# Modulation vector: four column quarters on the partitions

## Chip, cores and metric

The kernel runs on one core of one Trainium2 chip. The metric is device time in microseconds (us) from start to end of one launch, as the median of several runs; lower is better. Everything is fp32 at the interface.

## What is computed

Two transformer blocks on x of 256 tokens by 2048 features. The first has compressed, selected and windowed attention, a feed-forward layer of width 8192 and a gated embedding; the second has sliding-window and latent attention and again a feed-forward layer of width 8192. The second block is modulated by a conditioning vector c of 2048 elements. The part that the change touches:

```python
c_act = jax.nn.silu(c)                       # (1, 2048)
mod = c_act @ w_mod[l] + b_mod[l]            # w_mod: (2048, 6 * 2048), 96 MB
sh1, sc1, g1, sh2, sc2, g2 = [m[:, None, :] for m in jnp.split(mod, 6, axis=-1)]
h = rmsnorm(x, attn_norm_g[l]) * (1.0 + sc1) + sh1
...
x = x + g1 * jnp.einsum('bsm,md->bsd', mix, w_out[l])
h = rmsnorm(x, mlp_norm_g[l]) * (1.0 + sc2) + sh2
u = jax.nn.relu(jnp.einsum('bsd,df->bsf', h, w_ff1[l]))
x = x + g2 * jnp.einsum('bsf,fd->bsd', u * u, w_ff2[l])
```

`mod` does not depend on x, so its 96 MB of weights are read and summed during the first block, beside that block's matrix products.

## The kernel before

Each of the five engines has a program of its own, written by hand in the order in which it runs; semaphores order them against each other. There is no scheduler. SP (SyncE) issues nearly all loads, ACT and VectorE prepare the weights, TensorE (PE) multiplies.

**Weights of the products.** SP loads units of 1 MB (four blocks of 128 rows by 512 columns, rows of 2 KB) into four slots `raw`. A unit is two steps. For each step ACT copies 128x1024 elements to the rounded type (`upper`, L498) and VectorE subtracts that from the original (`lower`, L912), so that a product of two fp32 matrices can be made from three products of rounded halves. PE waits for `lower_ready`, multiplies a step (L1519 to L1521 in the form "tokens", L1530 and L1535 in the form "columns") and increments `step_used`, which frees the buffer of `upper` and `lower` four steps on. So ACT and VectorE run at most four steps ahead of PE. A product of 2048x512 weights is a group of 8 steps; SP loads the unit for a slot as soon as VectorE has made both `lower` halves of the unit that lay in it.

**The modulation.** w_mod is cut in 96 units of 128 rows by 2048 columns, 16 for each of the six sections. SP issues two units in a group of the first block, behind the third and the fourth load of `raw` (`mod_unit`, L313), alternately into the two slots of `modraw`; before that it waits until the unit two back has been added. VectorE adds a unit behind two of its eight `lower` operations (`add_mod`): the whole `modacc` of 128x2048 is multiplied by a pointer scalar of `silu_c` and added (L926; L924 for the first unit of a section, without the addition). After sixteen units `modacc` holds, on partition p, the sum over the rows with that p, for all 2048 columns of the section. PE turns it (`sum_mod`, L1594: 16 transposes of 128x128, called between two steps of a group of tokens), and VectorE sums the rows of the turned blocks in PSUM (`store_mod`, L939: two reduces of 128x1024), adds the bias (L942) and has the section as 128 partitions by 16 columns in `modcol`. One of the six sections is finished behind the first block's first products, four in its feed-forward layer and the gate, the last one in the second block's first products.

The groups with modulation work are 8 of the first product, 4 of w_out, 32 of the feed-forward layer and 4 of the gate: 48 groups, two units each. In the gate groups VectorE has more besides: `gated` and `regained` (L1333 to L1351) lie in its order between two `lower` operations, and an addition right behind them.

**The start.** Nine vectors (gains, c, b_mod) and two position tables are loaded as rows into `vrow`; PE turns them with three transposes (L1602) and VectorE copies the columns to `vcol` (L1093, L1094), from which `silu_c` is made.

Of the kernel before, what the change touches and what calls it, by code (L numbers as in the profile page):

```python
# [25 lines left out]
P = 128  # L26
# [26 lines left out]
MODS = 6 * KC  # L53

# [30 lines left out]
def program(nc, a):  # L85
    with ExitStack() as ctx:
# [36 lines left out]
        modacc = place("modacc", [P, D], at=M + 16384)  # L123
# [61 lines left out]
        COL = dict(mix=0, ffn=16, ple=32, attn=48, mlp=64, c=80, q=96, kv=99, b=P, k=P + 96, v=2 * P)  # L185
# [103 lines left out]
        def _(sp):  # L289
# [41 lines left out]
            for t in range(T):  # L331
                sp.dma_start(h[:, t, :], a["x"][0, t * P:(t + 1) * P, :]).then_inc(x_landed[t], 16)
            vecs = [(a["norm_mix"][0], 0, 0), (a["norm_ffn"][0], 16, 0), (a["norm_ple"][0], 32, 0),
                    (a["attn_norm_g_2"][0], 48, 0), (a["mlp_norm_g_2"][0], 64, 0), (a["c_2"][0], 80, 0),
                    (a["mla_q_norm_g_2"][0], 96, 0), (a["mla_kv_norm_g_2"][0], 99, 0),
# [5 lines left out]
            sp.dma_start(vrow[0:32, 2, :], a["nsa_cmp_pos_v"][0]).then_inc(rows_landed, 16)  # L341

# [3 lines left out]
            with loop(sp, c, 5, {lower_ready: 8, mod_added: 2}) as i:  # L346
                group(w_in, i * NW + 2 * NW, mods=section_rows(i * 2 + 4, 0))
# [16 lines left out]
            with loop(sp, c, NG - 1, {lower_ready: 8, mod_added: 2}) as i:  # L364
                group(w_out, i * NW + NW, mods=section_rows(i * 2 + 2, 1))
# [14 lines left out]
            with loop(sp, c, QUARTERS - 1, {lower_ready: 64, mod_added: 16}) as i:  # L380
# [3 lines left out]
            with loop(sp, c, NG, {lower_ready: 8, mod_added: 2}) as i:  # L384
                group(w_gate, i * NW, mods=section_rows(i * 2 + 8, 5))
# [91 lines left out]
        def _(act):  # L477
# [164 lines left out]
            nc.scalar.activation(silu_c[:], vcol[:, COL["c"]:COL["c"] + KC], ACT.Sigmoid).then_inc(c_sigmoid, 1)  # L642
# [253 lines left out]
        def _(dve):  # L896
# [19 lines left out]
            def add_mod(k):  # L916

                slot = st["mod"] % 2
                dve.wait_ge(mod_landed[slot], c.next(mod_landed[slot], 16))
                if st["mod"]:  # L920
                    dve.wait_ge(mod_added, c.at(mod_added))
                w, s = modraw[:, slot, :], silu_c[:, bass.ds(k, 1)]
                if isinstance(k, int) and k == 0:
                    op = nc.vector.tensor_scalar(modacc[:], w, s, None, ALU.mult)  # L924
                else:
                    op = nc.vector.scalar_tensor_tensor(modacc[:], w, s, modacc[:], ALU.mult, ALU.add)  # L926
                op.then_inc(mod_added, 1)
                c.next(mod_added)
                st["mod"] += 1

            def store_mod(m):
# [161 lines left out]
            nc.vector.tensor_copy(vcol[:, 0:100], ps[:, 0, 0:100])  # L1093
            nc.vector.tensor_copy(vcol[:, P:], ps[:, 0, P:2 * P + CMP_LEN]).then_inc(cols_ready, 1)  # L1094
# [4 lines left out]
            link(nc.vector.tensor_tensor(silu_c[:], silu_c[:], vcol[:, COL["c"]:COL["c"] + KC], ALU.mult))  # L1099
# [12 lines left out]
            def heads_out(parity, i):  # L1112
# [3 lines left out]
            per = {"steps": 16, "groups": 2, upper_ready: 16, half_copied: 2, mod_added: 4,  # L1116
                   mod_landed[0]: 32, mod_landed[1]: 32}
# [182 lines left out]
            def ffn(gain, modulated):  # L1300
# [6 lines left out]
                if modulated:  # L1307
                    per[dve_step] = 1
                    per.update({mod_landed[0]: 128, mod_landed[1]: 128, mod_added: 16, mod_summed: 1})
# [181 lines left out]
        def _(pe):  # L1491
# [109 lines left out]
            for j, n in ((0, 100), (1, P), (2, CMP_LEN)):  # L1601
                op = nc.tensor.transpose(ps[:, 0, j * P:j * P + n], vrow[0:n, j, :], ident[0:n, 0:n])  # L1602
# [9 lines left out]
            def sums_and_bias():  # L1612
                sum_mod(KC)
# [229 lines left out]
            def ffn(norms, modulated):  # L1843
                def between():
                    sum_mod(c.at("mods", 0))
# [40 lines left out]
            group(tokens, xs, n=320, between={1: lambda: sum_mod(6 * KC), 4: turn_modulation})  # L1886
# [127 lines left out]
```

## Time and profile before

| what | us |
|---|---|
| median of 3 runs (2274.2 to 2277.11) | 2275.6 |
| the profiled execution | 2274.36 |
| its span, first to last instruction | 2272.7 |
| PE busy in the span | 2202.8 |
| VectorE (DVE) busy in the span | 1512.4 |
| ACT busy in the span | 1012.2 |

The profile is of one execution. Its own time is 1.66 us above its span and 1.24 us below the median. PE is the matmul queue of TensorE, PEld its weight loads, which overlap; DVE is VectorE. In an entry of the timeline the first number is the start in us from the span's start, the second the duration of the entry (of all its instructions, where it ends in xN), and in square brackets stands how long the engine had been idle and what released it. "granted clock" is the share of TensorE's full clock; it is 0.991 in the mean.

### The profile page before, as it was taken

To read this page: it belongs to the slowest core of one execution; us is meant where nothing else is said; L and a number is where in the kernel's file an instruction comes from. 1 tells how busy PE (TensorE), PEld (TensorE's weight loads), DVE (VectorE), ACT (ScalarE), POOL (GpSimd) and SP (SyncE) were. 2 spreads that over 40 slices of the span, in tenths; PEclk is the share of its full clock that TensorE was granted. 3 is DMA by queue.
4 is the path that set the end of the run, shared out by engine and by line. 5 is a ranking of instruction groups with operands and counts; after the bars stand their busy time and mean duration, and the time that the engine had idled before them with its cause. 6 is when DMAs were issued, how large, how long until landed. Compare 5 with 4: busy or idle time off the path is not lost.

```text
span 2272.7 us, 29448 instructions
## 1 busy us (share of the span) xinstructions
PE 2202.8 (97%) x11458; PEld 1883.6 (83%) x11458; DVE 1512.4 (67%) x1456; ACT 1012.2 (45%) x1262; POOL 15.1 (1%) x40
## 2 busy tenths in 40 slices
PE   7999999999999999999999898999999999999997
PEld 6888888788888888888878697887888888888886
DVE  6676566777777677767778865557555555655655
ACT  5443364544344344344355544545444443443442
POOL 1000000000000000000000000000000000000000
PEclk9999999999999999999999999999999999999999
DMA  8775508777887877877867353355556656556553
GB/s 323 292 277 180 168 1 315 245 274 287 285 276 280 300 253 265 299 270 279 303 231 279 121 192 112 125 191 151 183 204 182 192 201 186 186 188 200 184 196 120
DMA packets 213106, 499.67 MB, mean 220 GB/s; under 512 B 10068, under 2 KB 12680, under 8 KB 199800
## 3 DMA queue, kind: packets, MB, share of 16 engines
q1 hardware_dynamic: 211528, 491.16, 63.3%
q0 software_dynamic: 1456, 6.72, 0.8%
q8 instruction: 96, 1.57, 0.3%
q14 instruction: 26, 0.21, 0.0%
HBM read 495.68 MB, written 2.17 MB: 219 GB/s over the span
## 4 chain that ended last, share of the span: by engine, by line
PE 60%; issue 36%; DVE 2%; ACT 1%; DMA 0%; SPq 0%; POOL 0%; DVEq 0%; ACTq 0%; POOLq 0%
PE ps L1530 17%; PE ps L1519 9%; PE ps L1520 9%; PE ps L1521 9%; PE ps L1535 9%; PE ps L1711 2%; PE ps L1767 1%; PE ps L1577 1%; PE ps L1630 1%; PE ps L1594 0%; PE ps L1717 0%; ACT prob L707 0%; PE ps L1768 0%; PE ps L1765 0%; DMA raw<-in_nsa_w_in_dram 0%
## 5 line engine op out<-in xcount | busy, mean ns | idle before, releaser
L912 DVE TENSOR_TENSOR lower<-raw,upper 128x1024 fp32r<-128x1024 f32 (+2 forms) x733 | 884.0, 1216 | 523.7 <-ACT upper L498 520.4
L498 ACT ACTIVATE upper<-raw 128x1024 fp32r<-128x1024 f32 (+2 forms) x733 | 769.0, 1054 | 951.8 <-PE ps L1521 529.2
L1530 PE MATMUL ps<-xs,upper 128*128 128x512 f32 x2688 | 676.1, 394 | 4.6 <-DVE h L1002 4.2
L1530 PEld LDWEIGHTS ps<-xs,upper 128*128 128x128 f32 x2688 | 484.7, 189 | 92.6 <-issue 5.0
L1519 PE MATMUL ps<-upper,hidden 128*128 128x512 f32 x1024 | 399.4, 390 | 0.0
L1520 PE MATMUL ps<-lower,hidden 128*128 128x512 f32 x1024 | 398.7, 389 | 0.0
L1521 PE MATMUL ps<-upper,hidden 128*128 128x512 f32 x1024 | 398.7, 389 | 0.0
L1535 PEld LDWEIGHTS ps<-xs,lower 128*128 128x128 f32 x2688 | 367.7, 191 | 26.3
L1535 PE MATMUL ps<-xs,lower 128*128 128x256 f32 x2688 | 375.7, 283 | 0.0
L1519 PEld LDWEIGHTS ps<-upper,hidden 128*128 128x128 f32 x1024 | 192.3, 188 | 40.3 <-DVE lower L912 0.9
L1521 PEld LDWEIGHTS ps<-upper,hidden 128*128 128x128 f32 x1024 | 192.3, 188 | 39.9
L1520 PEld LDWEIGHTS ps<-lower,hidden 128*128 128x128 f32 x1024 | 192.3, 188 | 39.4
L926 DVE SCALAR_TENSOR_TENSOR modacc<-modraw,silu_c,modacc 128x2048 f32<-128x2048 f32 x90 | 211.2, 2347 | 0.4
L1519 PE MATMUL ps<-upper,xs 128*128 128x512 f32 (+1 forms) x512 | 200.4, 391 | 3.1 <-DVE lower L912 1.9
L1521 PE MATMUL ps<-upper,xs 128*128 128x512 f32 (+1 forms) x512 | 198.0, 387 | 0.0
L1520 PE MATMUL ps<-lower,xs 128*128 128x512 f32 (+1 forms) x512 | 197.8, 386 | 0.0
L1519 PEld LDWEIGHTS ps<-upper,xs 128*128 128x128 f32 x512 | 96.7, 189 | 24.5 <-issue 4.1
L1521 PEld LDWEIGHTS ps<-upper,xs 128*128 128x128 f32 x512 | 96.6, 189 | 19.4
L1520 PEld LDWEIGHTS ps<-lower,xs 128*128 128x128 f32 x512 | 96.7, 189 | 18.2
L525 ACT ACTIVATE half<-ps 128x1024 f32<-128x1024 f32 x41 | 42.1, 1028 | 75.8 <-PE ps L1535 75.8
L979 DVE TENSOR_TENSOR summed<-ps,half 128x1024 f32<-128x1024 f32 x32 | 39.2, 1225 | 50.3 <-ACT half L525 50.3
L538 ACT ACTIVATE hidden<-summed 128x1024 fp32r<-128x1024 f32 x32 | 34.0, 1063 | 51.4 <-DVE summed L981 51.4
(260 smaller groups left out, 1165.7 us busy)
## 6 DMA issues: line engine op xcount, KB each, us to landing
raw<-in_ffn_w_dram SPq DMA_DIRECT2D x128, 1024.0 KB, 5.8
raw<-in_w_ff_dram SPq DMA_DIRECT2D x128, 1024.0 KB, 5.4
modraw<-in_w_mod_dram SPq DMA_DIRECT2D x96, 1024.0 KB, 7.5
raw<-in_nsa_w_in_dram SPq DMA_DIRECT2D x40, 1024.0 KB, 5.2
raw<-in_nsa_w_out_dram SPq DMA_DIRECT2D x16, 1024.0 KB, 7.1
raw<-in_ple_w_gate_dram SPq DMA_DIRECT2D x16, 1024.0 KB, 5.2
raw<-in_w_out_dram SPq DMA_DIRECT2D x16, 1024.0 KB, 5.1
raw<-in_w_in_dram SPq DMA_DIRECT2D x12, 1024.0 KB, 5.3
```

The costliest lines, as they stand in the source:

```text
L498: nc.scalar.activation(dst, src, ACT.Copy).then_inc(upper_ready, 1)
L525: nc.scalar.activation(half[:], ps[:, 4 * parity:4 * parity + 4, S:2 * S], ACT.Copy).then_inc(half_copied, 1)
L538: nc.scalar.activation(hidden[:, 4 * g:4 * g + 4, 0, :], summed[:], ACT.Copy).then_inc(hidden_upper, 1)
L912: nc.vector.tensor_tensor(low, src, up, ALU.subtract).then_inc(lower_ready, 1)
L926: op = nc.vector.scalar_tensor_tensor(modacc[:], w, s, modacc[:], ALU.mult, ALU.add)
L979: done(nc.vector.tensor_tensor(summed[:], ps[:, 4 * parity:4 * parity + 4, 0:S], half[:], ALU.add))
L1519: mm(out, xu, up[:, kk, :], start=first, stop=False)
L1520: mm(out, xu, low[:, kk, :], start=False, stop=False)
L1521: op = mm(out, xl, up[:, kk, :], start=False, stop=last)
L1530: mm(ps[:, 4 * par + f, :], up[:, kk, f * P:(f + 1) * P], both, start=(k == 0), stop=False, skip_group_check=True)
L1535: op = mm(ps[:, 4 * par + f, 0:S], low[:, kk, f * P:(f + 1) * P], x[:, k, 0, :], start=False, stop=(k == KC - 1), skip_group_check=True)
L1711: op = mm(out, q, k, start=first, stop=False, skip_group_check=True)
```

## The change

A unit of w_mod keeps its 128 rows by 2048 columns, but lies otherwise. Partitions 32q to 32q+31 now hold the column quarter q (512 columns) of all 128 rows: row 32m+b of the unit is on partition 32q+b, in part m of four parts of 512 elements each. So one unit is loaded by four DMAs of 32 partitions by 4 by 512 elements (256 KB each, rows of 2 KB) where one DMA of 128 partitions by 8 KB did it. An addition becomes four, of 128x512 elements, one for each part, each waiting for the one before and each with a column of `silu_c`; for that c is loaded so that column 4k+m holds elements 32m.. of unit k, repeated for the four quarters (64 columns where 16 were). `modacc` has 128x512 elements, a section's sum takes 4 transposes, all into PSUM bank 2, and one reduce of 128x512 to 128x16 over 32 elements each; the addition of the bias reorders the columns. The load of c moves from the sixth place among the eleven small loads to the last; it reads 64x4 rows of 32 elements. The counts of `mod_added` and `mod_landed` grow fourfold everywhere.

```diff
+PARTS = 4
+ROWS = P // PARTS
...
-        modacc = place("modacc", [P, D], at=M + 16384)
+        modacc = place("modacc", [P, D // PARTS], at=M + 16384)
...
-        vcol = place("vcol", [P, 2 * P + CMP_LEN])
+        vcol = place("vcol", [P, 2 * P + CMP_LEN + PARTS * KC])
...
-        modsum = place("modsum", [P, 2, KC // 2])
-        silu_c = place("silu_c", [P, KC])
+        modsum = place("modsum", [P, KC])
+        silu_c = place("silu_c", [P, PARTS * KC])
...
             def mod_unit(row, col):
                 slot = st["mod"] % 2
                 if st["mod"] >= 2:
-                    sp.wait_ge(mod_added, c.next(mod_added))
+                    sp.wait_ge(mod_added, c.next(mod_added, PARTS))
                 st["mod"] += 1
-                sp.dma_start(modraw[:, slot, :], w_mod[row, col]).then_inc(mod_landed[slot], 16)
+                src = w_mod[row, col].rearrange("(m b) (q n) -> q b m n", b=ROWS, q=PARTS)
+                for q in range(PARTS):
+                    dst = modraw[q * ROWS:(q + 1) * ROWS, slot, :].rearrange("b (m n) -> b m n", m=PARTS)
+                    sp.dma_start(dst, src[q]).then_inc(mod_landed[slot], 16)
...
+            rows_c = a["c_2"][0].rearrange("(m b) -> m b", b=ROWS).unsqueeze(1).to_broadcast([PARTS * KC, PARTS, ROWS])
+            sp.dma_start(vrow[CMP_LEN:CMP_LEN + PARTS * KC, 2, :].rearrange("m (q b) -> m q b", b=ROWS),
+                         rows_c).then_inc(rows_landed, 16)
...
             def add_mod(k):
 
                 slot = st["mod"] % 2
-                dve.wait_ge(mod_landed[slot], c.next(mod_landed[slot], 16))
-                if st["mod"]:
-                    dve.wait_ge(mod_added, c.at(mod_added))
-                w, s = modraw[:, slot, :], silu_c[:, bass.ds(k, 1)]
-                if isinstance(k, int) and k == 0:
-                    op = nc.vector.tensor_scalar(modacc[:], w, s, None, ALU.mult)
-                else:
-                    op = nc.vector.scalar_tensor_tensor(modacc[:], w, s, modacc[:], ALU.mult, ALU.add)
-                op.then_inc(mod_added, 1)
-                c.next(mod_added)
+                dve.wait_ge(mod_landed[slot], c.next(mod_landed[slot], 16 * PARTS))
+                for m in range(PARTS):
+                    if st["mod"] or m:
+                        dve.wait_ge(mod_added, c.at(mod_added))
+                    w, s = modraw[:, slot, m * NW:(m + 1) * NW], silu_c[:, bass.ds(k * PARTS + m, 1)]
+                    if isinstance(k, int) and k == 0 and m == 0:
+                        op = nc.vector.tensor_scalar(modacc[:], w, s, None, ALU.mult)
+                    else:
+                        op = nc.vector.scalar_tensor_tensor(modacc[:], w, s, modacc[:], ALU.mult, ALU.add)
+                    op.then_inc(mod_added, 1)
+                    c.next(mod_added)
                 st["mod"] += 1
...
-                for i, bank in enumerate((2, 6)):
-                    op = nc.vector.tensor_reduce(modsum[:, i], ps[:, bank:bank + 2, :].rearrange("p b (k n) -> p (b k) n", n=P),
-                                                 AX.X, ALU.add)
-                link(op)
-                nc.vector.tensor_tensor(dst, modsum[:].rearrange("p a k -> p (a k)"), b, ALU.add).then_inc(mod_stored, 1)
+                link(nc.vector.tensor_reduce(modsum[:], ps[:, 2, :].rearrange("p (k n) -> p k n", n=ROWS), AX.X, ALU.add))
+                by_part = lambda v: v.rearrange("p (q i) -> p i q", q=PARTS)
+                op = nc.vector.tensor_tensor(by_part(dst), modsum[:].rearrange("p (i q) -> p i q", q=PARTS), by_part(b), ALU.add)
+                op.then_inc(mod_stored, 1)
...
-                for k in range(KC):
-                    op = nc.tensor.transpose(ps[:, (2, 3, 6, 7)[k // 4], k % 4 * P:(k % 4 + 1) * P],
-                                             modacc[:, k * P:(k + 1) * P], ident[:])
+                for i in range(PARTS):
+                    op = nc.tensor.transpose(ps[:, 2, i * P:(i + 1) * P], modacc[:, i * P:(i + 1) * P], ident[:])
```

PE's order where the first section is summed, in the first group of tokens (`upper`, `lower` are the split weights, L1616 is the bias table's product). Before:

```order
L1519 MATMUL ps<-upper,xs 128x512
L1520 MATMUL ps<-lower,xs 128x512
L1521 MATMUL ps<-upper,xs 128x512
L1594 MATMUL ps<-ident,modacc 128x128 x16
L1616 MATMUL ps<-onehot,relb 16x128
```

The same place in the changed kernel:

```order
L1527 MATMUL ps<-upper,xs 128x512
L1528 MATMUL ps<-lower,xs 128x512
L1529 MATMUL ps<-upper,xs 128x512
L1602 MATMUL ps<-ident,modacc 128x128 x4
L1623 MATMUL ps<-onehot,relb 16x128
```

Nothing moved; twelve of the sixteen transposes are gone. The other places where a section is summed read the same way.

VectorE's order in a gate group, from the gated sum to the second addition (L1339 and L1351 are squares and the gain). Before:

```order
L1333 TENSOR_TENSOR half<-half,embed 128x1024
L1334 TENSOR_TENSOR h<-half,h 128x2x512
L912 TENSOR_TENSOR lower<-raw,upper 128x1024
L1339 ISA xn,sumsq<-h 128x512
L1339 ISA sumsq 128x1
L1351 TENSOR_TENSOR h<-h,gainrow 128x2x512
L1339 ISA xn,sumsq_114<-h 128x512
L1339 ISA sumsq_114 128x1
L926 SCALAR_TENSOR_TENSOR modacc<-modraw,silu_c,modacc 128x2048
L912 TENSOR_TENSOR lower<-raw,upper 128x1024 x3
L926 SCALAR_TENSOR_TENSOR modacc<-modraw,silu_c,modacc 128x2048
```

In the changed kernel:

```order
L1341 TENSOR_TENSOR half<-half,embed 128x1024
L1342 TENSOR_TENSOR h<-half,h 128x2x512
L920 TENSOR_TENSOR lower<-raw,upper 128x1024
L1347 ISA xn,sumsq<-h 128x512
L1347 ISA sumsq 128x1
L1359 TENSOR_TENSOR h<-h,gainrow 128x2x512
L1347 ISA xn,sumsq_114<-h 128x512
L1347 ISA sumsq_114 128x1
L935 SCALAR_TENSOR_TENSOR modacc<-modraw,silu_c,modacc 128x512 x4
L920 TENSOR_TENSOR lower<-raw,upper 128x1024 x3
L935 SCALAR_TENSOR_TENSOR modacc<-modraw,silu_c,modacc 128x512 x4
```

The order is the same; each addition is four instructions.

SP's order behind the small loads at the start (the first product's weights and the first units of w_mod). Before:

```order
L341 DMA vrow<-in_nsa_cmp_pos_v_dram 32x128
L306 DMA raw<-in_nsa_w_in_dram 128x4x512 x3
L313 DMA modraw<-in_w_mod_dram 128x2048
L306 DMA raw<-in_nsa_w_in_dram 128x4x512
L313 DMA modraw<-in_w_mod_dram 128x2048
```

In the changed kernel:

```order
L346 DMA vrow<-in_nsa_cmp_pos_v_dram 32x128
L348 DMA vrow<-in_c_dram 64x4x32
L308 DMA raw<-in_nsa_w_in_dram 128x4x512 x3
L318 DMA modraw<-in_w_mod_dram 32x4x512 x4
L308 DMA raw<-in_nsa_w_in_dram 128x4x512
L318 DMA modraw<-in_w_mod_dram 32x4x512 x4
```

Each unit of w_mod takes four issues, and the loads of `raw` behind it in SP's order come three issues later; the load of c is now the last of the eleven small ones.

## Rows read from the trace of the kernel before

**Rows 1.** The page: busy time, share of the span and instructions of each engine.

```profile
PE 2202.8 (97%) x11458; PEld 1883.6 (83%) x11458; DVE 1512.4 (67%) x1456; ACT 1012.2 (45%) x1262; POOL 15.1 (1%) x40
```

**Rows 2.** The page: the chain of work that ended last, shares by engine.

```profile
PE 60%; issue 36%; DVE 2%; ACT 1%; DMA 0%; SPq 0%; POOL 0%; DVEq 0%; ACTq 0%; POOLq 0%
```

**Rows 3.** Trace by tile modacc: durations min/median/max, starts.

```profile
L1594 PE MATMUL ps<-ident,modacc x96: 271/273/274, 205.4 to 1310.5; 128*128 128x128 f32 x96
L926 DVE SCALAR_TENSOR_TENSOR modacc<-modraw,silu_c,modacc x90: 2343/2347/2353, 37.4 to 1258.1; 128x2048 f32<-128x2048 f32 x90
L924 DVE TENSOR_SCALAR modacc<-modraw,silu_c x6: 1282/1286/1289, 36.0 to 1078.7; 128x2048 f32<-128x2048 f32 x6
```

**Rows 4.** Timeline, PE, 710 to 713 us: start, duration, what.

```profile
710.78 1.91 PE L1594 MATMUL ps<-ident,modacc 128*128 128x128 f32 x16
712.45 0.48 PE L1519 MATMUL ps<-upper,hidden 128*128 128x512 f32 x1
```

**Rows 5.** Timeline, VectorE, 712 to 718 us, after the same transposes.

```profile
712.73 2.36 DVE L939 TENSOR_REDUCE modsum<-ps 128x8 f32<-128x1024 f32 x2 [1.24 <-PE ps L1594]
...
715.56 1.29 DVE L924 TENSOR_SCALAR modacc<-modraw,silu_c 128x2048 f32<-128x2048 f32 x1
...
716.76 3.49 DVE L912 TENSOR_TENSOR lower<-raw,upper 128x1024 fp32r<-128x1024 f32 x3
```

**Rows 6.** VectorE's groups with shapes apart: count, busy us, mean ns, idle before.

```profile
L1229 DVE TENSOR_REDUCE stat<-ps 128x4 f32<-128x512 f32 x14 | 9.6, 686 | 6.4 <-PE ps L1717 4.7 <-PE ps L1723 1.7
L1046 DVE TENSOR_SCALAR xn<-h,norm 128x512 f32<-128x512 f32 x20 | 8.4, 483 | 0.2
...
L1082 DVE SCALAR_TENSOR_TENSOR h<-h,norm,gainrow 128x1024 f32<-128x1024 f32 x4 | 4.9, 1278 | 1.0 <-DMA gainrow<-in_final_norm_g_dram 1.0
```

**Rows 7.** Timeline, VectorE, two operations of which the second waits on the first.

```profile
1279.09 0.99 DVE L1063 TENSOR_SCALAR tmp<-ps,affine,modcol 128x256 f32<-128x256 f32 x2
1280.12 0.69 DVE L1067 TENSOR_TENSOR xs<-tmp,xs 128x512 fp32r<-128x512 f32 x1
```

**Rows 8.** Timeline, all engines, 1208 to 1212 us, a gate group.

```profile
1208.20 2.35 DVE L926 SCALAR_TENSOR_TENSOR modacc<-modraw,silu_c,modacc 128x2048 f32<-128x2048 f32 x1
...
1210.47 3.49 DVE L912 TENSOR_TENSOR lower<-raw,upper 128x1024 fp32r<-128x1024 f32 x3
...
1211.74 0.19 PEld L1519 LDWEIGHTS ps<-upper,xs 128*128 128x128 f32 x1 [0.45 <-DVE lower L912]
```

**Rows 9.** Busy time by stretch: PE, PEld, DVE, ACT, POOL, clock, DMA share, GB/s.

```profile
68.50:90.80 22.30, 22.30 (x130) 19.63 (x129) 15.16 (x13) 9.40 (x9) 0.00 (x0) 1.00 0.78 283
...
1200.00:1266.00 66.00, 65.93 (x288) 53.62 (x287) 56.30 (x52) 32.80 (x40) 0.00 (x0) 1.00 0.72 256
346.90:390.00 43.10, 43.10 (x193) 35.70 (x193) 33.37 (x25) 19.34 (x19) 0.00 (x0) 1.00 0.98 368
...
10.00:32.00 22.00, 16.94 (x97) 15.17 (x98) 17.89 (x35) 15.02 (x28) 0.00 (x0) 1.00 1.04 396
```

**Rows 10.** DMA issues by line: count, KB each, median us from issue to landing.

```profile
raw<-in_ffn_w_dram SPq DMA_DIRECT2D x128, 1024.0 KB, 5.8
...
modraw<-in_w_mod_dram SPq DMA_DIRECT2D x96, 1024.0 KB, 7.5
...
prow<-in_p_dram POOLq DMA_DIRECT2D x1, 256.0 KB, 3.3
```

**Rows 11.** Timeline, ACT and VectorE, 356 to 365 us, first groups of w_out.

```profile
356.99 1.06 ACT L498 ACTIVATE upper<-raw 128x1024 fp32r<-128x1024 f32 x1 [3.07 <-DMA raw<-in_nsa_w_out_dram]
...
363.74 1.23 DVE L1002 TENSOR_TENSOR h<-ps,h 128x1024 f32<-128x1024 f32 x1 [0.34 <-PE ps L1521]
```

**Rows 12.** Timeline, 11 to 16 us: the vectors turned into columns.

```profile
11.40 0.85 PE L1602 MATMUL ps<-ident,vrow 100*128 100x100 f32 x3 [11.40 <-DMA vrow<-in_nsa_cmp_pos_v_dram]
...
13.25 2.00 ACT L498 ACTIVATE upper<-raw 128x1024 fp32r<-128x1024 f32 x2 [1.18 <-DMA raw<-in_nsa_w_in_dram]
...
14.06 0.32 DVE L1094 COPY vcol<-ps 128x160 f32<-128x160 f32 x1
```

More of the change, by code:

```diff
@@ L341, in _ @@
             sp.dma_start(vrow[0:32, 2, :], a["nsa_cmp_pos_v"][0]).then_inc(rows_landed, 16)
+            rows_c = a["c_2"][0].rearrange("(m b) -> m b", b=ROWS).unsqueeze(1).to_broadcast([PARTS * KC, PARTS, ROWS])
+            sp.dma_start(vrow[CMP_LEN:CMP_LEN + PARTS * KC, 2, :].rearrange("m (q b) -> m q b", b=ROWS),
+                         rows_c).then_inc(rows_landed, 16)
             group(w_in, 0, mods=[mods_of(0), mods_of(1)])
             group(w_in, NW, mods=section_rows(2, 0))
-            with loop(sp, c, 5, {lower_ready: 8, mod_added: 2}) as i:
+            with loop(sp, c, 5, {lower_ready: 8, mod_added: 2 * PARTS}) as i:
                 group(w_in, i * NW + 2 * NW, mods=section_rows(i * 2 + 4, 0))
@@ L363, in _ @@
                 mod_unit(*rows_cols)
-            with loop(sp, c, NG - 1, {lower_ready: 8, mod_added: 2}) as i:
+            with loop(sp, c, NG - 1, {lower_ready: 8, mod_added: 2 * PARTS}) as i:
                 group(w_out, i * NW + NW, mods=section_rows(i * 2 + 2, 1))
@@ L379, in _ @@
             quarter(ffn1, ffn2, 0, quarter_mods(0))
-            with loop(sp, c, QUARTERS - 1, {lower_ready: 64, mod_added: 16}) as i:
+            with loop(sp, c, QUARTERS - 1, {lower_ready: 64, mod_added: 16 * PARTS}) as i:
                 quarter(ffn1, ffn2, i + 1, quarter_mods(i + 1))
@@ L383, in _ @@
                 unit(w_embed[:, 0:2, u * 1024:(u + 1) * 1024], 2, 1024)
-            with loop(sp, c, NG, {lower_ready: 8, mod_added: 2}) as i:
+            with loop(sp, c, NG, {lower_ready: 8, mod_added: 2 * PARTS}) as i:
                 group(w_gate, i * NW, mods=section_rows(i * 2 + 8, 5))
@@ L640, in _ @@
             to_features(vcol[:, COL["mix"]:COL["mix"] + KC], ahead=2)
-            nc.scalar.activation(silu_c[:], vcol[:, COL["c"]:COL["c"] + KC], ACT.Sigmoid).then_inc(c_sigmoid, 1)
+            nc.scalar.activation(silu_c[:], vcol[:, COL["c"]:COL["c"] + PARTS * KC], ACT.Sigmoid).then_inc(c_sigmoid, 1)
             group([first_half])
@@ L1092, in _ @@
             dve.wait_ge(rows_turned, 1)
[L1093 to L1094 removed]
+            nc.vector.tensor_copy(vcol[:, 0:84], ps[:, 0, 0:84])
+            nc.vector.tensor_copy(vcol[:, P:], ps[:, 0, P:2 * P + CMP_LEN + PARTS * KC]).then_inc(cols_ready, 1)
             dve.wait_ge(cols_ready, 1)
@@ L1115, in _ @@
             group([heads_out(0, 0)], mods=2)
-            per = {"steps": 16, "groups": 2, upper_ready: 16, half_copied: 2, mod_added: 4,
-                   mod_landed[0]: 32, mod_landed[1]: 32}
+            per = {"steps": 16, "groups": 2, upper_ready: 16, half_copied: 2, mod_added: 4 * PARTS,
+                   mod_landed[0]: 32 * PARTS, mod_landed[1]: 32 * PARTS}
             with loop(dve, c, 3, per) as i:
@@ L1308, in ffn @@
                     per[dve_step] = 1
-                    per.update({mod_landed[0]: 128, mod_landed[1]: 128, mod_added: 16, mod_summed: 1})
+                    per.update({mod_landed[0]: 128 * PARTS, mod_landed[1]: 128 * PARTS, mod_added: 16 * PARTS, mod_summed: 1})
                 with loop(dve, c, QUARTERS - 1, per) as i:
@@ L1600, in _ @@
             pe.wait_ge(rows_landed, 16 * 11)
-            for j, n in ((0, 100), (1, P), (2, CMP_LEN)):
+            for j, n in ((0, 84), (1, P), (2, CMP_LEN + PARTS * KC)):
                 op = nc.tensor.transpose(ps[:, 0, j * P:j * P + n], vrow[0:n, j, :], ident[0:n, 0:n])
@@ L1612, in sums_and_bias @@
             def sums_and_bias():
-                sum_mod(KC)
+                sum_mod(PARTS * KC)
                 pe.wait_ge(aux_landed, 16 * 5)
@@ L1844, in between @@
                 def between():
-                    sum_mod(c.at("mods", 0))
+                    sum_mod(PARTS * c.at("mods", 0))
                     c.next("mods", KC)
@@ L1885, in _ @@
             group_turned(tokens, 3)
-            group(tokens, xs, n=320, between={1: lambda: sum_mod(6 * KC), 4: turn_modulation})
+            group(tokens, xs, n=320, between={1: lambda: sum_mod(6 * PARTS * KC), 4: turn_modulation})
             group(columns, xs, between={4: turn_latents})
```

8 lines of the change are left out of this document (4 added, 4 removed).

## The prediction, made before the changed kernel ran

> **What bounds the kernel now.** I read the page's busy times first [rows 1]: PE is busy for 2202.8 of 2272.7 us, VectorE for 1512.4, ACT for 1012.2. The chain that ended last [rows 2] says the same: 60% PE and 36% "issue", which is PE's own stream between matmuls, VectorE 2%, ACT 1%, DMA 0%. So an instruction taken out of PE's stream is worth its whole spacing, and work on VectorE or on the DMA engines costs nothing until it makes PE wait. Then I read the stretches in which the modulation is made [rows 9]: in an ordinary group of the first product (68.5 to 90.8 us) VectorE is busy for 15.16 of 22.3 us and the DMA engines for 0.78 of the time, at 283 GB/s; behind the attention (346.9 to 390 us) the DMA engines are busy for 0.98; in the gate groups (1200 to 1266 us) VectorE is busy for 56.30 of 66 us. These are the places where the cover is thin. Last the single waits: the one in a gate group [rows 8], the one for w_out's weights [rows 11] and the one at the start [rows 12].
>
> **The transposes.** Sixteen of them take 1.91 us from first start to last end [rows 4], but the next matmul starts 1.67 us after the first of them, so one is worth 1.67/16 = 0.104 us of PE's stream; the 273 ns of [rows 3] are the length of a pipelined one. Twelve fewer are 1.25 us, and over six sections 7.5 us. That is on the path: PE does not wait before or behind them in the place shown. In the last section, with short steps, PE is as busy, so I take 1.25 us there too.
>
> **The sum behind them.** VectorE reads the turned blocks in PE's way: two reduces, a bias addition, the first unit of the next section, and only then the `lower` that PE wants two steps on [rows 5]. Before: from 712.73 to 716.76, 4.03 us to the start of `lower`, whose first part ends near 718.0, just when PE gets there. After: one reduce of 512 elements, for which the nearest row is 0.69 us [rows 6], saves 2.36 - 0.69 = 1.67 us; the first unit becomes one plain multiplication of 512 elements, 0.48 us [rows 6], and three additions, which cost 1.5 us more (worked out below). The two cancel to 0.1 us and I book 0. If the quarter additions cost more than I take, PE waits here in four of the sections (up to 0.3 us each for every 0.1 us that I am off per addition).
>
> **The additions.** The trace has no addition of 512 elements with a pointer scalar. It has the same instruction at 2048 elements, 2347 ns [rows 3], and at 1024, 1278 ns [rows 6]; the slope is 1.044 ns an element, so 512 cost 1278 - 535 = 743 ns. An operation that waits on its forerunner starts about 0.04 us after its end (1279.09 + 0.99 = 1280.08, next start 1280.12 [rows 7]). Four cost 4 x 0.743 + 3 x 0.04 = 3.09 us in place of 2.35, +0.74 us; the bounds are 4 x 0.48 (the plain one) = 1.9 us, below what stands there now, and 4 x 1.278 = 5.1 us. I take 3.09, since it is between two rows of the very instruction. A section's first unit costs 0.48 + 3 x 0.78 = 2.8 us in place of 1.29. Over the span: 90 x 0.74 + 6 x 1.5 = 76 us more on VectorE, less 6 x 1.67 = 10 us.
>
> What covers this: in the ordinary group 2 x 0.74 = 1.5 us go on top of 15.16 of 22.3 us [rows 9], and VectorE is four steps ahead of PE, so nothing reaches PE. In the gate groups it does. There the first addition stands ahead of the `lower` that PE takes next [rows 8]: the addition starts at 1208.20, `lower` at 1210.47, and PE's weight load, at 1211.74, has already been idle for 0.45 us with VectorE as its releaser. The margin is gone before the change, so 0.74 us go straight into PE's stream, in each of the three gate groups that are built like this: +2.2 us. The second addition stands between steps for which PE is not yet there. Queued behind the longer additions are the `lower` operations, and who waits for them is PE; for the release of a `modraw` slot SP waits, but it comes to that wait only when a unit of `raw` has been freed, two steps after the addition.
>
> **The loads.** This is the cost that the trace of before can't price. 96 transfers become 384, each to 32 partitions, in rows of 2 KB in place of 8 KB. Rows of 2 KB alone are harmless: the feed-forward weights have them and land in 5.8 us where a unit of w_mod takes 7.5 [rows 10], and a queue that is full moves 396 GB/s with both kinds in it (10 to 32 us [rows 9]), 2.65 us for 1 MB. For 32 partitions at this size there is no row. One bound is 2.65 us a unit, no loss. The other is four transfers that don't overlap at all: the 256 KB of `prow` land in 3.3 us [rows 10], 13.2 us a unit. That end has a reason against it: between 10 and 32 us eight megabytes from many transfers went through at full rate, so a queue overlaps its transfers. Whether PE feels it depends on one sum. A group of 22.0 us (three gate groups are 66 us, one of the first product 22.3 [rows 9]) needs four units of `raw`, 10.6 us, and two of w_mod, so the cover lasts until a unit of w_mod takes (22.0 - 10.6)/2 = 5.7 us. I take the lower end for the forecast, the nearest to rows with many transfers in flight, and keep what lies above as rivals.
>
> On this the Trainium skill has a rule that speaks against the change. "SBUF — State Buffer", section "Door 1: The DMA port swizzle", says that a transfer reaches only the ports of its own partitions, eight of sixteen for 32 partitions, and gives 189 GB/s for partitions 0 to 31 against 328 for all 128 at 1 MB; the section after it says that transfers to different parts don't add up. By that a unit takes 2.35 us longer, 5.0 us by an estimate from that page, and the DMA engines are full for 94% of a group. No row here shows it.
>
> **Small things.** The issue of three more DMAs delays SP, which waits for slots most of the time. The columns at the start: PE waits for the last small load until 11.40, VectorE has the columns at 14.38, ACT needs them when it is through with two `upper` at 15.25 [rows 12]. There are 0.9 us for a load of c that now comes last and in rows of 128 bytes; I book 0, with 0.5 us as its bound.
>
> **The sum.** -7.5 + 2.2 + 0 + 0 = -5.3 us. On the profiled execution's own figures: span 2272.7 - 5.3 = 2267.4, plus 1.66 around it, 2269.1. The median of the runs lies 1.24 us higher, so I predict 2270.3.
>
> **Rivals.** (1) A load to 32 partitions runs at half the rate, 5.3 us a unit. A group then needs 10.6 + 10.6 = 21.2 of 22.0 us, which is still covered. But behind the attention, where the queue is full already (0.98 [rows 9]), two units of w_mod stand ahead of the weights for which ACT waited 3.07 us at 356.99 [rows 11]. They would come 5.3 us later: `upper` from 362.3, `lower` done near 364.7, while PE ended its group at about 363.7 [rows 11]. PE waits 1 us there and perhaps 1 to 4 more for the next ones, since the queue no longer catches up. I put 3 us: -2.3 us in all, 2273.3. The port rule of the skill's page just named would give this case. For it: nothing else in the kernel has this shape. Against: no row.
>
> (2) The slower side: a unit of w_mod takes more than 5.7 us, 46% of the full queue's rate. From there the DMA engines set the pace of all 48 groups with modulation work, since four slots of `raw` don't bridge a lasting deficit. At 40% of the rate, 6.6 us, a group lasts 23.8 us, +1.8 us, +86 us in all with the forecast's -5.3: 2356. At a third, 8 us, it is +4.6 us a group and some 2490. For it: 0.98 behind the attention, and 0.78 already in an ordinary group, so little is missing. Against: the queue's 396 GB/s show that small pieces are moved at full rate.
>
> (3) The quarter additions cost more than 0.74 us, for instance 1.3 us at the price of an instruction that can't be overlapped with its wait. The gate groups give 3 x 1.3 = 3.9 us, the four sums in the feed-forward layer some 1.5 us each: -7.5 + 3.9 + 6 = +2.4, 2278.0. Against: [rows 7] show a short gap.
>
> (4) The change gives more: PE loses less than 0.74 us in the gate groups since VectorE catches up, 2268.
>
> **Chances.** Forecast 0.42, rival (1) 0.25, (2) 0.18, (3) 0.09, (4) 0.06. About 0.2%, 4.5 us, is what a measurement of this kernel can tell from no change. Faster by more: most of the forecast (0.34), (4) and a little of (1) (0.04): 0.44. Slower by more: (2) with 0.18 and most of (3), 0.07, and the tail of (1), 0.02: 0.27. The same: 0.29. The range: the low end is all 7.5 us of the transposes and 1 us of waits, 2267. At the high end I leave out the larger part of rival (2), 0.13, and about 0.05 at the low end: 2300.
>
> **What would show it.** Right: four transposes in 0.5 us and their successor 0.42 us behind the first; a 512-element addition of 0.74 us; PE's weight load in the gate groups idle for about 1.2 us where it was 0.45; ACT's waits for `raw` as before. Rival (1): w_mod's landing well above 7.5 us, ACT and then PE waiting for `raw` between 355 and 365 us. Rival (2): DMA share above 0.95 in all stretches with modulation, and PE waiting in each group. The forecast is wrong if PE's idle time grows anywhere outside the gate groups by more than 2 us.

## The result, and the profile after

The changed kernel takes 2352.0 us (median of 4 runs, 2344.1 to 2375.4) against 2274.9 us for the kernel before (4 runs): a ratio of 1.035, with an interval of 1.031 to 1.039. It is 77 us slower where I forecast 5 us faster. The profiled execution has a span of 2342.4 us, 69.7 us more than before.

The page of the changed kernel: busy times, then the line of the queue that carries the loads (packets, MB, share), then the chain of work that ended last by engine and by line. They answer to [rows 1, 2].

```profile
PE 2222.2 (95%) x11386; PEld 1889.8 (81%) x11386; DVE 1564.0 (67%) x1738; ACT 1008.2 (43%) x1262; POOL 15.2 (1%) x40
...
q1 hardware_dynamic: 253240, 491.20, 73.9%
...
issue 38%; PE 29%; DMA 18%; DVE 10%; SPq 3%; ACT 1%; DVEq 0%; POOL 0%; ACTq 0%; POOLq 0%
DMA modraw<-in_w_mod_dram 17%; PE ps L1538 8%; PE ps L1543 4%; DVE modacc L935 4%; PE ps L1527 4%; PE ps L1529 4%; PE ps L1528 4%; DVE lower L920 3%; SPq L318 3%; PE ps L1718 2%; DMA raw<-in_nsa_w_in_dram 2%; PE ps L1585 1%; PE ps L1774 1%; PE ps L1637 1%; SPq L308 0%
```

PE's share of the chain has halved, and the loads of w_mod, which were nowhere in it, are its longest piece. The queue moves the same 491 MB, but its packets take 73.9% of the span. Before, the queue's line reads:

```profile
q1 hardware_dynamic: 211528, 491.16, 63.3%
```

The stretches of [rows 9] in the changed kernel (columns as there: PE, PEld, DVE, ACT, POOL, clock, DMA share, GB/s), and one long stretch of the feed-forward layer:

```profile
68.50:90.80 22.30, 18.08 (x90) 15.50 (x89) 12.59 (x14) 7.72 (x8) 0.00 (x0) 0.85 1.00 254
...
45.00:200.00 155.00, 147.20 (x817) 128.53 (x816) 102.92 (x108) 59.11 (x58) 0.00 (x0) 0.97 1.01 264
...
900.00:1100.00 200.00, 184.52 (x901) 154.65 (x900) 142.05 (x147) 74.53 (x73) 0.00 (x0) 0.97 0.96 254
```

The same long stretch of the kernel before:

```profile
900.00:1100.00 200.00, 197.76 (x997) 167.99 (x996) 149.11 (x112) 82.46 (x79) 0.00 (x0) 1.00 0.80 283
```

This is the reading that decides. The packets now fill nearly all of the DMA engines' time, and they move less: 254 GB/s at a share of 0.96 where 283 GB/s took 0.80. (The share adds up the times of the packets, so it can pass 1.) A group with modulation moves six units of 1.049 MB, 6.29 MB; at 264 GB/s, the rate from 45 to 200 us, that is 23.8 us, where PE needs 22.0. The rate is not the same everywhere: 272 GB/s from 500 to 700 us, 254 from 900 to 1100.

Who waits for it, in the changed kernel (total us, times, longest), and how long a transfer takes from issue to landing, which answers to [rows 10]:

```profile
ACT upper L506 <- DMA raw<-in_ffn_w_dram: 176.6, 46, 7.5
...
DVE modacc L935 <- DMA modraw<-in_w_mod_dram: 103.4, 43, 7.2
ACT upper L506 <- DMA raw<-in_nsa_w_in_dram: 93.9, 25, 12.4
```

```profile
raw<-in_ffn_w_dram SPq DMA_DIRECT2D x128, 1024.0 KB, 14.7
raw<-in_w_ff_dram SPq DMA_DIRECT2D x128, 1024.0 KB, 5.3
modraw<-in_w_mod_dram SPq DMA_DIRECT2D x384, 256.0 KB, 9.2
```

The unchanged loads of the feed-forward weights land after 14.7 us in place of 5.8 [rows 10]: they stand behind w_mod in the same queue. The second feed-forward layer, without modulation work, has 5.3 us, and had 5.4. The loss is confined to where w_mod is loaded: the last transpose of `modacc` starts at 1310.5 us in the kernel before and at 1380.1 us now, 69.6 us later, and the whole span is 69.7 us longer.

Some waits of PE cost more than their length. Timeline of the changed kernel, PE's first matmuls after its waits, and the stretch around the second by pieces of 4 us (columns as in [rows 9]):

```profile
65.69 2.11 PE L1538 MATMUL ps<-xs,upper 128*128 128x512 f32 x8 [1.45 <-DVE lower L920]
84.14 3.78 PE L1538 MATMUL ps<-xs,upper 128*128 128x512 f32 x8 [4.22 <-DVE lower L920]
```

```profile
80.00:84.00 4.00, 0.00 (x0) 0.00 (x0) 3.54 (x5) 1.30 (x2) 0.00 (x0) 0.76 1.05 334
84.00:88.00 4.00, 3.86 (x10) 3.08 (x11) 2.68 (x4) 0.71 (x1) 0.00 (x0) 0.50 0.67 189
88.00:92.00 4.00, 4.00 (x25) 3.68 (x25) 3.56 (x5) 1.07 (x1) 0.00 (x0) 0.89 1.07 306
```

After 1.45 us of idle time eight matmuls take 2.11 us. After 4.22 us the granted clock is 0.50, the lower of TensorE's two levels (1.2 GHz), and the same eight take 3.78 us; it had fallen while PE stood still (0.52 from 82 to 84 us) and is 1.00 again from 90 to 92 us. The length of the wait alone doesn't decide it: after 2.00 us (before 754.54) the granted clock is 0.50 too, after 3.14 us (before 1026.03) it is 0.90. Over the span PE is idle for 2342.4 - 2222.2 = 120.2 us against 69.9 before, 50.3 us more; by the other 19.4 of the 69.7 us PE is busy for longer, though 72 transposes are gone. Against a_oneload below, which has the same instructions on PE and a clock of 0.990, PE is busy for 26.1 us longer (2222.2 against 2196.1) in a span that is 73.6 us longer. The mean granted clock falls from 0.991 to 0.980.

### The profile page after: what moved, and what is told of

Its sections match the earlier page's. It is cut to its first block, busy times and chain, and to the rows that moved or that the text cites. A ratio compares the mean times of both kernels' runs of the same rounds, so it can differ in the third digit from the quotient of the medians.

```text
span 2342.4 us, 30373 instructions
## 1 busy us (share of the span) xinstructions
PE 2222.2 (95%) x11386; PEld 1889.8 (81%) x11386; DVE 1564.0 (67%) x1738; ACT 1008.2 (43%) x1262; POOL 15.2 (1%) x40
## 3 DMA queue, kind: packets, MB, share of 16 engines
q1 hardware_dynamic: 253240, 491.20, 73.9%
## 4 chain that ended last, share of the span: by engine, by line
issue 38%; PE 29%; DMA 18%; DVE 10%; SPq 3%; ACT 1%; DVEq 0%; POOL 0%; ACTq 0%; POOLq 0%
DMA modraw<-in_w_mod_dram 17%; PE ps L1538 8%; PE ps L1543 4%; DVE modacc L935 4%; PE ps L1527 4%; PE ps L1529 4%; PE ps L1528 4%; DVE lower L920 3%; SPq L318 3%; PE ps L1718 2%; DMA raw<-in_nsa_w_in_dram 2%; PE ps L1585 1%; PE ps L1774 1%; PE ps L1637 1%; SPq L308 0%
## 5 line engine op out<-in xcount | busy, mean ns | idle before, releaser
L1538 PE MATMUL ps<-xs,upper 128*128 128x512 f32 x2688 | 685.3, 397 | 23.0 <-DVE lower L920 22.5
L1538 PEld LDWEIGHTS ps<-xs,upper 128*128 128x128 f32 x2688 | 489.7, 191 | 115.3 <-DVE lower L920 25.9
L935 DVE SCALAR_TENSOR_TENSOR modacc<-modraw,silu_c,modacc 128x512 f32<-128x512 f32 x378 | 284.0, 751 | 118.0 <-DMA modraw<-in_w_mod_dram 103.4
L1529 PEld LDWEIGHTS ps<-upper,xs 128*128 128x128 f32 x512 | 97.4, 190 | 19.8
## 6 DMA issues: line engine op xcount, KB each, us to landing
raw<-in_ffn_w_dram SPq DMA_DIRECT2D x128, 1024.0 KB, 14.7
```

Source lines behind the costliest of these rows:

```text
L1529: op = mm(out, xl, up[:, kk, :], start=False, stop=last)
L1538: mm(ps[:, 4 * par + f, :], up[:, kk, f * P:(f + 1) * P], both, start=(k == 0), stop=False, skip_group_check=True)
```

## The experiments

The theories on the loads: **N**, a transfer to 32 neighbouring partitions is slow (and, as **P**, what counts is the part of SBUF that a transfer reaches); **R**, rows of 2 KB are slow; **C**, four transfers in place of one are slow; beside them **V**, that VectorE's longer work is the cause. In the ratios of the experiments the runs of before are those made on the same chip (medians 2275.7, 2276.2 and 2278.1 us in the three sets). Beside each change of the loads shown here, the counts that VectorE waits for grow or shrink with the number of transfers. The landing time is that of one transfer, so it can be compared only between transfers of the same size (1 MB, or 512 or 256 KB where a unit is split in two or four).

| kernel | transfer of a unit of w_mod | median us | ratio to before, interval | landing of one transfer, us |
|---|---|---|---|---|
| changed | 4, 32 neighbours, 2 KB | 2352.0 | 1.035 (1.031 to 1.039) | 9.2 |
| b_rows32 | 4, 32 neighbours, 8 KB | 2353.4 | 1.036 (1.033 to 1.038) | 10.0 |
| b_rows64 | 2, 64 neighbours, 8 KB | 2350.2 | 1.033 (1.032 to 1.035) | 12.1 |
| b_step2 | 2, every second partition, 8 KB | 2277.1 | 0.9998 (0.9989 to 1.0007) | 6.5 |
| b_cols4 | 4, all 128, 2 KB | 2277.7 | 1.0004 (0.9994 to 1.0014) | 5.8 |
| b_half | every second unit as b_rows32 | 2278.7 | 1.0014 (1.0005 to 1.0023) | 7.5 (narrow), 11.4 (wide) |
| a_alt | changed, order 0, 2, 1, 3 | 2306.4 | 1.014 (1.011 to 1.016) | 9.6 |
| a_oneload | changed, 1, all 128, 8 KB | 2271.0 | 0.9977 (0.9967 to 0.9986) | 7.4 |
| b_fewer | before with 4 of 16 transposes | 2269.5 | 0.9961 (0.9948 to 0.9975) | 7.6 |
| a_step4 | changed, 4, every fourth, 2 KB | 2268.9 | 0.9967 (0.9956 to 0.9978) | 5.4 |
| a_gate | a_step4, additions moved | 2265.5 | 0.9952 (0.9938 to 0.9966) | 5.4 |
| a_bym | a_gate, 4, all 128, 2 KB | 2267.0 | 0.9949 (0.9936 to 0.9963) | 5.5 |

**Narrow transfers alone (b_rows32).**

```diff
-sp.dma_start(modraw[:, slot, :], w_mod[row, col]).then_inc(mod_landed[slot], 16)
+for q in range(4):
+    sp.dma_start(modraw[32 * q:32 * q + 32, slot, :],
+                 w_mod[row, col][32 * q:32 * q + 32, :]).then_inc(mod_landed[slot], 16)
```

> The kernel before with one edit: each unit of w_mod (128 partitions, rows of 8 KB) is loaded by four transfers, each to 32 neighbouring partitions, rows still 8 KB. Transposes, additions and values are those of before. Theory N (a transfer to 32 neighbouring partitions is slow, and four of them in turn do not make up for it): a unit takes about 6.6 us of the DMA engines as in the changed kernel, so the 48 groups with modulation last about 23.7 us in place of 22.0: 2275 + 82 = about 2357 us, DMA share about 1.0 in all stretches with modulation at some 265 GB/s. Theory R (the rows of 2 KB are what is slow): 2275, nothing changes here. Theory C (four transfers in place of one, whatever their shape): about 2357 here as well, told from N by the next kernel. Theory V (VectorE's longer work holds PE back): 2275.

2353.4 us. The whole loss is there in the kernel before, with its own transposes, additions and 8 KB rows. R and V are out as causes of the loss; N and C are left. Busy time in the feed-forward layer (columns as in [rows 9]):

```profile
500.00:700.00 200.00, 196.24 (x1006) 167.65 (x1005) 145.70 (x109) 80.78 (x79) 0.00 (x0) 0.99 0.99 271
```

**Four wide transfers in rows of 2 KB (b_cols4).**

```diff
+for q in range(4):
+    sp.dma_start(modraw[:, slot, NW * q:NW * q + NW],
+                 w_mod[row, col][:, NW * q:NW * q + NW]).then_inc(mod_landed[slot], 16)
```

> The kernel before with one edit: each unit of w_mod is loaded by four transfers of 512 columns each to all 128 partitions, so rows of 2 KB, the number of transfers and the size of rows as in the changed kernel, but every transfer spans all partitions. Theory N (narrow ranges of partitions): 2275, within 3 us, DMA share in an ordinary group near 0.8 as before. Theories R (2 KB rows) and C (four transfers): about 2350, DMA share near 1.0.

2277.7 us, no difference. The same stretch, and the page's line of the queue:

```profile
500.00:700.00 200.00, 200.00 (x1040) 171.67 (x1039) 149.80 (x112) 85.38 (x82) 0.00 (x0) 1.00 0.83 284
```

```profile
q1 hardware_dynamic: 253000, 491.18, 64.1%
```

It has as many packets as the changed kernel (253,000 against 253,240) and as many transfers, but its packets take 64.1% of the span and not 73.9. C and R fall; N stands.

**Everything but the loads (a_oneload).** The changed kernel with the one wide load of before.

> The changed kernel with one edit: a unit of w_mod is loaded by one transfer to 128 partitions in rows of 8 KB, as before the change. The modulation's values are computed from a wrong arrangement of w_mod; the instructions of every engine are those of the changed kernel. It prices everything in the change but the loads. My forecast for that was -5.3 us against before (-7.5 for the transposes, +2.2 for the additions in the gate groups): 2269.6. Theory V (additions and the longer section's first unit cost PE more): above 2275. If the additions cost nothing in the gate groups: 2267.4.

2271.0 us against 2275.7, -5.2 us by the ratio (-7.5 to -3.2). The forecast for the rest of the change was -5.3. V falls a second time: with VectorE's longer work in place and wide loads there is no loss.

**The same narrow count, spread (a_step4).**

```diff
-dst = modraw[q * ROWS:(q + 1) * ROWS, slot, :].rearrange("b (m n) -> b m n", m=PARTS)
+dst = modraw[q::PARTS, slot, :].rearrange("b (m n) -> b m n", m=PARTS)
 ...
-ps[:, 2, :].rearrange("p (k n) -> p k n", n=ROWS)
+ps[:, 2, :].rearrange("p (i b q) -> p i q b", b=ROWS, q=PARTS)
 ...
+nc.vector.tensor_copy(vrow[0:PARTS * KC, 4, :].rearrange("m (b q) -> m b q", q=PARTS),
+    vrow[0:PARTS * KC, 3, 0:ROWS].unsqueeze(2).to_broadcast([PARTS * KC, ROWS, PARTS])).then_inc(c_spread, 1)
```

> The changed kernel with another arrangement: column quarter q of row b stands on partition 4b+q and not 32q+b, so each of the four transfers of a unit goes to 32 partitions again, but to every fourth one over the whole width. The columns of c are spread to match by one more copy on VectorE at the start, and the row sum reads with a stride of four. 96 KB of difference in nothing else. Theory N-range (what is slow is a transfer that reaches only a quarter of the partitions' range): the loads are as fast as before, and the time is 2269 to 2272. Theory N-count (what is slow is 32 partitions or rows of 2 KB or four transfers, wherever they lie): about 2350.

2268.9 us, faster than before. (The phrase on 96 KB in that text was a slip and means nothing.) Each transfer still fills 32 partitions with rows of 2 KB, and a unit still takes four; only which partitions has changed, by which 83 us are gone. The source of each transfer (`src[q]`) is the same too, so where the bytes are read from is not the cause. Not the number of partitions counts but where they lie. The queue's line in this kernel, where the changed one had 253,240 packets and 73.9%:

```profile
q1 hardware_dynamic: 253048, 491.18, 64.2%
```

**64 neighbours against every second partition (b_rows64, b_step2).** Two transfers each, to `modraw[64 * q:64 * q + 64]` and to `modraw[q::2]`.

> The kernel before with one edit: each unit of w_mod is loaded by two transfers, to partitions 0 to 63 and 64 to 127, rows of 8 KB. Four transfers to 32 neighbours each (b_rows32) gave 2353 us. Theory P (what counts is which part of SBUF a transfer reaches, and 64 neighbours reach no more than 32 do): a unit is as slow as in four pieces, about 2350 us, DMA share about 1.0. Theory W (the rate goes with the number of neighbouring partitions): 64 are about half way, a unit takes (2.65 + 6.55)/2 = 4.6 us, which is below the 5.7 us that a group covers: 2276 to 2280 us, DMA share near 0.9. The Trainium skill, 'SBUF - State Buffer', section 'Door 1: The DMA port swizzle', says that partitions 0 to 63 reach the same eight ports as 0 to 31, which would be theory P.

> The kernel before with one edit: each unit of w_mod is loaded by two transfers of 64 partitions, the even and the odd ones, rows of 8 KB. It differs from b_rows64 (2350 us) only in which 64 partitions a transfer takes. Theory P (which part of SBUF a transfer reaches): every second partition reaches all of it, so 2276, DMA share 0.8 in an ordinary group. If any transfer to 64 partitions were slow: 2350.

2350.2 and 2277.1 us. Twice as many neighbours buy nothing; spreading them buys all of it. The runs hold only which partitions a transfer fills; that 0 to 63 reach the same eight ports as 0 to 31 is what the Trainium skill says ("SBUF — State Buffer", section "Door 1: The DMA port swizzle"), and both results are as that rule has them. No run here shows the ports themselves.

**Another order (a_alt).** `for q in (0, 2, 1, 3)` in place of `range(PARTS)`.

> The changed kernel with one edit: the four transfers of a unit are issued in the order 0, 2, 1, 3 in place of 0, 1, 2, 3, so that two transfers issued one behind the other go to different halves of the partitions. Theory O (transfers in flight at the same time overlap, and are slow here only because neighbours in the queue reach the same part of SBUF): the loads speed up towards the full rate; where a unit comes below 5.7 us, the time falls to 2270 to 2275. Theory S (each narrow transfer is slow by itself and they follow one another on the same DMA engines): 2350, as the changed kernel.

2306.4 us, between the two theories: 46 of the 77 us are gone. The loads themselves became only a little faster: 274 GB/s in place of 264 from 45 to 200 us, 272 in place of 254 from 900 to 1100. So little is worth so much because the changed kernel is only just past what a group covers. That transfers to different halves overlap in part would explain the gain, but no run shows the overlap itself. Neither theory is right by itself; spreading each transfer does what the order does only in part. The stretch from 500 to 700 us in this kernel:

```profile
500.00:700.00 200.00, 200.00 (x1033) 171.46 (x1032) 160.76 (x165) 86.06 (x83) 0.00 (x0) 1.00 1.05 283
```

The share is 1.05 and PE never stops. A share near 1 is therefore no proof by itself that PE waits for the loads; the rate beside it has to be too low as well (283 GB/s is what PE takes here, the changed kernel has 272).

**Half of the units narrow (b_half).**

```diff
+for q in range(1 if slot else 4):
+    f = slice(0, P) if slot else slice(32 * q, 32 * q + 32)
+    sp.dma_start(modraw[f, slot, :], w_mod[row, col][f, :]).then_inc(mod_landed[slot], 16)
```

> The kernel before with one edit: only every second unit of w_mod (those in slot 0 of modraw) is loaded by four transfers to 32 neighbouring partitions each, rows of 8 KB; the others by one. It tests the threshold of the prediction, 5.7 us a unit. A group then needs 4 x 2.65 + 2.65 + 6.55 = 19.8 us of the DMA engines out of 22.0. Threshold right: no group is paced by the loads, only the stretch behind the attention may lose a few us: 2275 to 2280, DMA share about 0.9 in an ordinary group. Threshold wrong (the cost is felt in proportion to the slow units): half of the 78 us, 2314.

2278.7 us, +3.2 (1.1 to 5.2) and not half of the loss. The loss is no sum over slow transfers: half of the units narrow cost 3 us, all of them 78. The queue still had air in the stretch of before:

```profile
500.00:700.00 200.00, 200.00 (x1038) 171.66 (x1037) 149.61 (x113) 85.43 (x82) 0.00 (x0) 1.00 0.90 283
```

The share was 0.80 with no narrow unit, is 0.90 with one of two (I had 19.8/22.0 = 0.90), and PE never stops in this stretch. What little is lost lies behind the attention: from 432 to 500 us PE is busy for 64.3 us, before for 67.3. The queue's packets take 0.674 x 2277.1 = 1535 us in place of 0.633 x 2272.7 = 1439, so 48 narrow units cost 96 us more packet time, 2.0 us each. With the 2.65 us of a wide one that is about 4.7 us, an estimate.

**The transposes alone (b_fewer).** The kernel before with `for k in (0, 4, 8, 12)` in front of the transposes.

> The kernel before with one edit: only 4 of the 16 transposes of a section are made, so PE's stream is 72 transposes shorter; loads, additions and both reduces are those of before, and the reduces read what is left in the other blocks (the modulation's values are incomplete). It measures the first term of my sum by itself: 12 x 0.104 us in each of six sections, 7.5 us, so 2268.7. If PE waits behind the transposes for something else in some sections, less: 2270 to 2274.

2269.5 us, -8.9 us by the ratio (-11.8 to -5.7) where I had -7.5.

**The additions in the gate groups (a_gate).**

```diff
 for g in range(1, NG):
-    group([gated(g - 1), regained(g - 1)], mods=8 + 2 * g)
+    group([gated(g - 1), regained(g - 1)], mods=8 + 2 * g, at=(4, 6))
```

> a_step4 (2268.9 us) with one more edit: in the three gate groups the first of the two additions stands one step later on VectorE, behind the `lower` that PE takes next and not ahead of it. In a_step4 PE's weight load was idle for 1.21 us there, with VectorE as its releaser, where the kernel before had 0.45. If the additions of the gate groups stand on the path as I said, 3 x 1.2 = 3.6 us come back: 2265.3. If the wait only moves to the next `lower`: 2268.9. If SP, which waits for the addition before it loads the next unit, now comes late: 2270 or more, with waits of ACT for raw in the gate groups.

2265.5 us. PE's weight loads that waited for VectorE's `lower`, first in a_step4 and then in a_gate (total us, times, longest):

```profile
PEld ps L1530 <- DVE lower L920: 4.1, 6, 1.2
```

```profile
PEld ps L1530 <- DVE lower L920: 0.5, 3, 0.2
```

3.6 us of wait of the weight loads have gone, as expected. PE's matmuls got back less: between 1150 and 1330 us their waits for `lower` fall from 4.3 to 1.9 us, and the two spans (2264.2 and 2263.2) differ by 1.0. The intervals of the two kernels overlap, and they ran on different chips, so that 2265.5 meets the forecast of 2265.3 is partly luck; by times alone the gain is not settled.

**Wide transfers for the same arrangement (a_bym).** One transfer for each set of 32 rows, `modraw[:, slot, m * NW:(m + 1) * NW]`.

> a_gate (2265.5 us) with other transfers: partition 4b+q as there, but a unit is cut by its four sets of 32 rows, so each of the four transfers fills all 128 partitions with 2 KB each. Theory P: both reach all of SBUF and the loads are covered in both, so 2265.5 within 2 us. If a transfer to 32 spread partitions still cost something that the cover hides only in part, this one is faster, 2263 to 2264, and the landing of w_mod shorter than 5.4 us.

2267.0 us, w_mod lands after 5.5 us: no different from a_gate. Both are faster than the kernel before, by 0.5%, and than the changed one.

## Why the prediction was wrong

**The loads: the step that failed.** I booked 0 for them, with 2.65 us a unit as the nearest row's price, since a full queue had moved 396 GB/s in many transfers. Those transfers all filled 128 partitions, so the row bore on the number of transfers and on 2 KB rows (b_cols4 says that it was right there) and not on narrow ones, of which the trace had none. The pace of the changed kernel gives 6.29 MB / 264 GB/s = 23.8 us a group, so (23.8 - 10.6)/2 = 6.6 us a unit; by the rates of the two later stretches it is 6.3 and 7.1 us. Over all 48 groups the span is 73.6 us longer than that of a_oneload, 1.53 us a group, which gives 6.5 us a unit. What came was rival (2), a unit above 5.7 us and the loads setting the pace, with its signs: DMA share above 0.95 in most of the stretches, PE waiting. That its example of 6.6 us and 2356 us came so close to 2352.0 is partly luck: it named 8 us and 2490 us as well, and the pace varies between the stretches. It had 0.18 and the range left most of it out. Its chance was too low because I counted the 396 GB/s as evidence against it.

**The threshold.** That there is a point up to which the group covers the loads was right in kind (b_half: 0.90, nothing lost in an ordinary group). The price to hold against it was not one number. A narrow unit costs about 4.7 us while the queue has air (b_half), by which the all-narrow kernel would need 10.6 + 9.4 = 20.0 of 22.0 us, and yet it is paced. The cheapness of 2.65 us was part of the error: from 500 to 700 us a group of before has the DMA engines busy for 0.80 x 22.0/6 = 2.9 us a unit, and 17.6 us plus twice 2.0 are already 21.6 of 22.0 us. In the changed kernel the packets take longer still: (0.739 x 2342.4 - 1439)/96 = 3.0 us more for each narrow unit in place of 2.0. That packet time is not the whole of it either: a_alt has nearly as much (0.742 x 2301.0 = 1707 us against 1731) and is 46 us faster. What sets the price of a narrow transfer between the two stays open. Rival (1), which held a half-rate load of 5.3 us a unit to be covered, did not come either: the loads did not stay at that price.

The Trainium skill's figures ("SBUF — State Buffer", section "Door 1: The DMA port swizzle"), from which I worked out 5.0 us a unit and 94% of a group, come close to the 4.7 us of b_half; the changed kernel shows that an estimate of 94% was no cover. The prediction's sentence on transfers to different parts draws on the Trainium skill, "SBUF — State Buffer", section "Can I just issue two DMAs to hit both halves?", which gives +6% for two of them against one. The gain in rate of a_alt is of that size (4 and 7% in the two stretches above); what the runs add is that so small a gain can be worth 46 us.

**Behind the transposes.** Four transposes and their successor, in a_step4 (the same instructions without the loads' waits); they answer to [rows 4, 5]:

```profile
710.10 0.60 PE L1605 MATMUL ps<-ident,modacc 128*128 128x128 f32 x4
...
710.45 0.48 PE L1530 MATMUL ps<-upper,hidden 128*128 128x512 f32 x1
...
710.73 0.69 DVE L947 TENSOR_REDUCE modsum<-ps 128x16 f32<-128x512 f32 x1
...
711.90 0.49 DVE L933 TENSOR_SCALAR modacc<-modraw,silu_c 128x512 f32<-128x512 f32 x1
...
712.42 2.33 DVE L935 SCALAR_TENSOR_TENSOR modacc<-modraw,silu_c,modacc 128x512 f32<-128x512 f32 x3
```

The successor starts 0.35 us behind the first transpose (expected 0.42), so 1.32 us are saved in this section; the six save 1.30 to 1.32 us each, 7.9 us in all, where 7.5 was forecast. Reduce 0.69 and first product 0.49 us are as taken. The `lower` behind them starts at 714.66, 3.93 us after the reduce (4.03 before), so the two changes cancel to 0.1 us as worked out. The load of c, booked at 0 with a bound of 0.5 us, cost nothing: PE's first wait ends at 11.26 us in the changed kernel and at 11.40 before.

**The additions.** Durations min/median/max in the changed kernel, which answer to [rows 3]:

```profile
L935 DVE SCALAR_TENSOR_TENSOR modacc<-modraw,silu_c,modacc x378: 743/752/756, 37.7 to 1332.1; 128x512 f32<-128x512 f32 x189
```

I had 743 ns; four in a row take 3.11 us (expected 3.09). And the weight load in the gate group, in a_step4, which answers to [rows 8]:

```profile
1203.74 0.19 PEld L1530 LDWEIGHTS ps<-upper,xs 128*128 128x128 f32 x1 [1.21 <-DVE lower L920]
```

1.21 us where 0.45 stood. The matmul there starts 1.17 us after its forerunner, in the kernel before 0.41 us (1211.33 to 1211.74): 0.76 us went straight into PE's stream, as said. The weight loads of the three gate groups waited for `lower` for 1.3 us before and for 3.6 us in a_step4, 2.3 us more where 2.2 was forecast. The line of the kernel before for 1150 to 1320 us (total us, times, longest):

```profile
PEld ps L1519 <- DVE lower L912: 1.3, 3, 0.4
```

Rivals (3) and (4) are out.

**The sum without the loads.** -5.3 against -5.2 measured (a_oneload). That interval (-7.5 to -3.2) is too wide to test single terms; the rows do that. Both terms with a row near their own instruction came out within half a microsecond (7.9 for 7.5, 2.3 for 2.2); the one without a row decided the sign.

## What to carry to other kernels

When an edit splits a transfer by partitions, ask not how many partitions each piece fills but whether it spans all of them: here pieces of every second or every fourth partition cost nothing and pieces of 32 or 64 neighbours 3.3 to 3.6%. Where a price has no row, a row of another shape is not evidence for the cheap end. Be wary of a queue that is nearly full on paper: here 90% of a group cost 3 us in all and an estimated 94% cost 77. Look at the DMA share and the GB/s together: a share that rises while the rate falls shows slow transfers, not more work, and a share of 1.05 with the rate that PE needs cost nothing.

## What the runs showed that I had not expected

That order alone gives back more than half (2352 to 2306 us when transfers of different halves alternate); that a narrow unit takes more packet time in a full queue (3.0 us extra) than in one with air (2.0 us); and that a wait of 4.2 us was followed by half the granted clock and made the next eight matmuls 1.7 us longer. In the profiled execution 26 of the 74 us by which it is longer than a_oneload are not idle time of PE but time in which PE is busy, at a lower mean clock.
